# Retention rows turned in 32x32 blocks by VectorE during attention, in place of TensorE transposes in the output projection

## The reference

```python
ret = head_norm(ret).reshape(b, l, RET_HEADS * RET_DV) * jax.nn.silu(rg)
fox = forgetting_attention(heads(fq, FOX_HEADS), heads(fk, FOX_HEADS), heads(fv, FOX_HEADS), pad(logf))[:, PAD:]
mixed = jnp.concatenate([ret, fox], axis=-1).astype(h.dtype)      # 512 + 512 wide
return jnp.einsum('blc,cd->bld', mixed, w_out)
# then: h = layer_norm(ALPHA * h + that); router, shared expert, routed experts (top 6 of 64), layer norm
```

## Time and profile before

| | |
|---|---|
| median of 3 runs | 2919.52 us |
| the profiled execution | 2925.15 us |
| its span, first to last instruction | 2923.2 us |
| mean granted TensorE clock | 0.994 of full |
| TensorE busy | 2845.5 us, 97% |
| VectorE busy | 1679.1 us, 57% |
| ScalarE busy | 626.5 us, 21% |
| GpSimd busy | 1348.8 us, 46% |
| moved by DMA | 462.10 MB, mean 158 GB/s |

### The profile page before, as it was taken

The page is one execution under the profiler, slowest core; times in us unless marked ns, Lnnn a source line. Parts: engine busy times, 40 slices in busy tenths (PEclk is TensorE's granted clock), DMA queues, the critical chain, the costliest instruction groups (busy, mean ns, idle before and its releaser), DMA issues.

```text
span 2923.2 us, 40626 instructions
## 1 busy us (share of the span) xinstructions
PE 2845.5 (97%) x14506; PEld 2078.4 (71%) x14506; DVE 1679.1 (57%) x4553; ACT 626.5 (21%) x1285; POOL 1348.8 (46%) x1140
## 2 busy tenths in 40 slices
PE   8999999999999999998999999999999999999997
PEld 4478888888875555554555767778877777777775
DVE  6665556654246666664577644677677773332326
ACT  2221122120015455543111100111111111111114
POOL 3433534447740110101245435677667766555645
PEclk9999999999999999999999999999999999999999
DMA  6500110101020103003543466899899989999986
GB/s 221 183 6 1 31 45 1 30 15 44 15 88 7 54 8 117 13 7 125 187 152 119 154 225 204 268 280 276 270 279 284 292 277 307 301 306 305 315 256 254
DMA packets 181019, 462.10 MB, mean 158 GB/s; under 512 B 26072, under 2 KB 98600, under 8 KB 155080
## 3 DMA queue, kind: packets, MB, share of 16 engines
q1 hardware_dynamic: 133872, 339.23, 32.3%
q0 software_dynamic: 44640, 111.84, 16.6%
q10 hardware_dynamic: 2304, 8.39, 0.7%
HBM read 345.44 MB, written 113.92 MB: 157 GB/s over the span
## 4 chain that ended last, share of the span: by engine, by line
PE 39%; DMA 7%; DVE 3%; POOL 2%; issue 1%; ACT 0%; SPq 0%; DVEq 0%; POOLq 0%; ACTq 0%
PE ps L3005 17%; PE ps L2775 8%; DMA moe_xg<-t_rows,index 6%; PE ps L2948 4%; PE ps L2919 3%; PE ps L2831 2%; DVE moe_xT L2060 2%; PE ps L2916 2%; POOL moe_xg L2484 1%; DMA base_rows<-moe_yo,index 1%; PE ps L2841 1%; PE ps L2794 1%; POOL moe_fin L2566 1%; PE ps L2785 0%; DVE moe_yo L2115 0%
## 5 line engine op out<-in xcount | busy, mean ns | idle before, releaser
L2484 POOL DMA_INDIRECT moe_xg<-t_rows,index x433 | 422.7, 976 | 166.9 <-issue 119.8
L3005 PEld LDWEIGHTS ps<-moe_xT,moe_wg 128*128 128x128 f32 x2048 | 352.4, 196 | 49.4 <-issue 28.4
L3005 PE MATMUL ps<-moe_xT,moe_wg 128*128 128x192 f32 (+22 forms) x2048 | 378.7, 338 | 4.7 <-DVE moe_hh L1960 4.7
L3005 PE MATMUL ps<-moe_xT,moe_wu 128*128 128x192 f32 (+22 forms) x2048 | 375.3, 336 | 0.0
L2505 POOL DMA_INDIRECT base_rows<-moe_yo,index x100 | 235.9, 2359 | 266.5 <-DVE moe_yo L2074 124.1
L3005 PEld LDWEIGHTS ps<-moe_xT,moe_wu 128*128 128x128 f32 x2048 | 353.3, 196 | 4.3
L2060 DVE STREAM_TRANSPOSE moe_xT<-moe_xg 128x256 f32<-128x256 f32 x433 | 235.1, 609 | 189.2 <-DMA moe_xg<-t_rows,index 159.3
L1274 POOL TENSOR_TENSOR fox_diag<-fox_c,fox_causal 128x128 f32<-128x128 f32 x128 | 55.8, 458 | 449.7 <-DVE fox_mx L1303 444.9
L2625 ACT ACTIVATE moe_sl<-ps 128x256 f32<-128x256 f32 (+19 forms) x144 | 49.8, 346 | 917.3 <-PE ps L3005 827.7
L1297 DVE CUSTOM_DVE_ANT_0 hT<-ps,fox_c 128x512 f32<-128x512 f32 (+7 forms) x320 | 166.4, 560 | 67.1 <-PE ps L1543 66.8
L2115 DVE SCALAR_TENSOR_TENSOR moe_yo<-ps,weight,moe_yo 128x512 f32<-128x512 f32 (+14 forms) x280 | 187.5, 742 | 28.3 <-ACT moe_yo L2648 28.3
(11 more groups left out here) (371 smaller groups left out, 5035.8 us busy)
## 6 DMA issues: line engine op xcount, KB each, us to landing
moe_wg<-in_we_gate SPq DMA_DIRECT2D x64, 1024.0 KB
moe_wu<-in_we_up SPq DMA_DIRECT2D x64, 1024.0 KB
moe_wd<-in_we_down SPq DMA_DIRECT2D x64, 1024.0 KB, 8.9
fox_c<-ck SPq DMA_DIRECT2D x8, 1032.0 KB, 8.9
emb_xin<-in_x SPq DMA_DIRECT2D x16, 512.0 KB, 3.9
h_rows<-emb_hr SPq DMA_DIRECT2D x16, 512.0 KB, 2.8
ret_w<-in_w_in SPq DMA_DIRECT2D x16, 512.0 KB, 6.6
moe_yt<-h_rows SPq DMA_DIRECT2D x16, 512.0 KB, 4.8
```

What stands on the lines that cost most here:

```text
L2484: pool.indirect_dma_start(out=xg[g % NXG][:, :], out_offset=None, in_=quarters, in_offset=bass.IndirectOffsetOnAxis(ap=route.index4[:, AT4 ...
L3005: ins = pe.matmul(out, w[:, c, f:FF:FC], xT[u][:, c, 0:n], start=(c == 0), stop=(c == DC - 1))
```

## The change

The transposes of the retention rows leave TensorE and the output projection. During attention, in the first four tiles of each pair (`TURN_AT`), the 16 blocks are turned one by one: SP loads the rows of a block in four pieces, one for each head, onto four bands of 32 partitions (`rows_to_turn`); VectorE turns them in blocks of 32x32 with one instruction (`turn_rows`); SP stores the result in a new DRAM array `mT_rows`. Turning by bands of 32 leaves features 4p to 4p + 3 on partition p, not p, p + 128, ...; the first half of `w_out` is loaded in that order (`quartered`). The projection then loads `mT` straight from `mT_rows`. `turn_mix` and `mT_copy` are gone, and `mixes(i + 3)` stands right behind `feathers(i + 3)`.

```diff
             def projection_weights():
-                natural = w_out.rearrange("(c p) n -> p c n", p=P)
+                quartered = w_out[0:RH * RD, :].rearrange("(p c) n -> p c n", c=RH)
+                natural = w_out[RH * RD:MIX, :].rearrange("(c p) n -> p c n", p=P)
...
+                sp.wait_ge(rows_out, 16 * 2)
                 for b in range(2):
-                    sp.dma_start(ahead.mix[b][:, :], mixed[P * b:P * (b + 1), :]).then_inc(ahead.mix_in[b], 16)
+                    sp.dma_start(ahead.mT[b][:, :, :], mT_rows[b].rearrange("p (c t) -> p c t", c=RH)).then_inc(ahead.mix_in[b], 16)
+
+            def rows_to_turn(m):
+                for h in range(RH):
+                    sp.dma_start(ahead.turn_in[QP * h:QP * (h + 1), :, :],
+                                 mixed[P * m:P * (m + 1), RD * h:RD * (h + 1)].rearrange("(g t) d -> t g d", t=QP)
+                                 ).then_inc(rows_in, 16)
...
+            sp.wait_ge(added, PRODUCTS * len(FUNITS))
+            rows_to_turn(0)
             pair_gates(1)
             for n, (p, t) in enumerate(order):
+                if n in TURN_AT:
+                    m = TURN_AT[n]
+                    sp.wait_ge(rows_turned, m + 1)
+                    sp.dma_start(mT_rows[m], flat(ahead.turn_out[:, :, :])).then_inc(rows_out, 16)
+                    if m + 1 < NX:
+                        rows_to_turn(m + 1)
                 if n == 2 * TILES + 1:
                     projection_weights()
...
+            def turn_rows(m):
+                dve.wait_ge(rows_in, 16 * RH * (m + 1))
+                if m >= 1:
+                    dve.wait_ge(rows_out, 16 * m)
+                dve.transpose(ahead.turn_out[:, :, :].rearrange("p c (g t) -> p g c t", t=QP),
+                              ahead.turn_in[:, :, :].rearrange("p g (t c) -> p g c t", c=RH)).then_inc(rows_turned, 1)
...
                     if i == 1 and n >= 1:
                         finish(n - 1)
+                    if i == 2 and n in TURN_AT:
+                        turn_rows(TURN_AT[n])
...
             def mixes(i):
-                if i >= 2:
-                    sp.wait_ge(mturned, i - 1)
-                sp.dma_start(mix[i % 2][:, :], rows(mixed, i)).then_inc(mix_in[i % 2], 16)
+                sp.wait_ge(projected, 2 * (i - 2) + 2)
+                sp.dma_start(mT[i % 2][:, :, :], mT_rows[i].rearrange("p (c t) -> p c t", c=RH)).then_inc(mix_in[i % 2], 16)
...
-            mixes(2)
             sp.dma_start(sgu[:, :, 0:FF], natural(ws_gate)).then_inc(sw_s, 16)
...
                     feathers(i + 3)
+                    mixes(i + 3)
                     hidden(i + 3)
-                if i + 4 < NX:
-                    mixes(i + 4)
...
             def project(i, a):
                 if a == 0:
-                    pe.wait_ge(mT_a, i + 1)
+                    pe.wait_ge(mix_in[i % 2], 16 * (i // 2 + 1))
...
             def rank(i):
                 pe.wait_ge(chain, chosen_at[i])
-                pe.wait_ge(mT_a, min(i + 5, NX))
...
                     pe.wait_ge(counted_in, i)
+                    pe.wait_ge(slotted, i)
...
-            turn_mix(0)
             for i in range(-2, NX - 2):
                 project(i + 2, 0)
                 if i >= 0:
                     turn_t(i)
-                if i < 0:
-                    turn_mix(i + 3)
                 project(i + 2, 1)
-                if 0 <= i < NX - 3:
-                    turn_mix(i + 3)
```

More of the change, by code:

```diff
@@ L222, in __init__ @@
         sb = Area(nc, "moe", (self.rows, self.small))
-        self.mix = [sb(f"mix{b}", [P, RH * RD]) for b in range(2)]
+        self.mT = [sb(f"mT{b}", [P, RH, P]) for b in range(2)]
+        self.turn_in, self.turn_out = sb("turn_in", [P, NQ, P]), sb("turn_out", [P, RH, P])
         self.base, self.wo_at = self.rows, self.low
@@ L1099, in retention_phase, with fox_phase @@
         yield
-def fox_phase(nc, ps, ident, hT, square, w_in, w_out, v_rows, ck, mixed, foxT, ahead):
+def fox_phase(nc, ps, ident, hT, square, w_in, w_out, v_rows, ck, mixed, mT_rows, foxT, ahead):
     with Phase(nc, "fox") as ph:
@@ L1193, in fox_phase @@
         ahead.fox_proj, ahead.q_scaled, ahead.fox_wsum, ahead.fox_tsum = proj, zero("q_scaled"), zero("wsum"), zero("tsum")
+        rows_in, rows_turned, rows_out = zero("rows_in"), zero("rows_turned"), zero("rows_out")
+        TURN_AT = {TILES * p + x: TILES // 2 * p + x for p in range(PAIRS) for x in range(TILES // 2)}
         scored, biased, bounded, exped, diag_set = (zero(n) for n in ("scored", "biased", "bounded", "exped", "diag_set"))
@@ L1223, in projection_weights @@
             def projection_weights():
[L1224 removed]
+                quartered = w_out[0:RH * RD, :].rearrange("(p c) n -> p c n", c=RH)
+                natural = w_out[RH * RD:MIX, :].rearrange("(c p) n -> p c n", p=P)
                 sp.wait_ge(scored, unit0[2 * TILES])
                 for a in range(2):
[L1227 to L1228 removed]
+                    half = slice(a * BANK, (a + 1) * BANK)
+                    sp.dma_start(ahead.wo[:, 0:RH, half], quartered[:, :, half]).then_inc(ahead.wo_s[a], 16)
+                    sp.dma_start(ahead.wo[:, RH:MIX // P, half], natural[:, :, half]).then_inc(ahead.wo_s[a], 16)
+                sp.wait_ge(rows_out, 16 * 2)
                 for b in range(2):
[L1230 removed]
+                    sp.dma_start(ahead.mT[b][:, :, :], mT_rows[b].rearrange("p (c t) -> p c t", c=RH)).then_inc(ahead.mix_in[b], 16)
[4 more added lines that the diff above has]
+                                 ).then_inc(rows_in, 16)
             sp.wait_ge(proj, pair_done(0))
@@ L1685, in __init__, with moe_phase @@
         self.ones_set = ctx.enter_context(nc.semaphore("ones_set"))
-def moe_phase(nc, ps, mixed, foxT, h_rows, w_out, ln_g, ln_b, w_router, router_bias, ws_gate, ws_up, ws_down,
+def moe_phase(nc, ps, mT_rows, foxT, h_rows, w_out, ln_g, ln_b, w_router, router_bias, ws_gate, ws_up, ws_down,
               we_gate, we_up, we_down, t_rows, tT_rows, base_rows, table, route, ln2_g, ln2_b, out, square, ahead):
@@ L1769, in moe_phase @@
         zrow = sb("zrow", [P, D])
-        mix = ahead.mix
+        mT = ahead.mT
         fT = [sb(f"fT{b}", [P, PAIRS, P]) for b in range(2)]
         rows0 = spans[-2] - 4 * PAIRS * P
-        mT = [sb(f"mT{b}", [P, RH, P]) for b in range(2)]
         tT = [sb(f"tT{b}", [P, DC, P]) for b in range(2)]
@@ L1820, in moe_phase @@
         t_out, tT_out, scat = ph.zero_sems("t_out", NYT), ph.zero_sems("tT_out", 2), ph.zero_sems("scat", 2)
-        mturned, mT_a, projected, summed, stats, aggr, centred, epsd, rstds, t_ready = (
-            zero(n) for n in ("mturned", "mT_a", "projected", "summed", "stats", "aggr", "centred", "epsd", "rstds", "t_ready"))
+        projected, summed, stats, aggr, centred, epsd, rstds, t_ready = (
+            zero(n) for n in ("projected", "summed", "stats", "aggr", "centred", "epsd", "rstds", "t_ready"))
         halved, halved_c, fold_set = (zero(n) for n in ("halved", "halved_c", "fold_set"))
@@ L3059, in build @@
     mixed, foxT = dram("mixed", (SEQ, RH * RD)), dram("foxT", (FH * FD, SEQ))
+    mT_rows = dram("mT_rows", (NX, P, RH * P))
     t_rows, base_rows = dram("t_rows", (SEQ + SPARE, D)), dram("base_rows", (SEQ + SPARE, D))
@@ L3069, in build @@
                   retention_phase(nc, ps, ident, hT, a["square"], a["w_in"], a["retc"], v_rows, ck, mixed, ahead),
-                  fox_phase(nc, ps, ident, hT, a["square"], a["w_in"], a["w_out"], v_rows, ck, mixed, foxT, ahead)]
+                  fox_phase(nc, ps, ident, hT, a["square"], a["w_in"], a["w_out"], v_rows, ck, mixed, mT_rows, foxT, ahead)]
         for stage in stages:
@@ L3077, in build @@
         route = Route(nc, ctx, ident)
-        moe_phase(nc, ps, mixed, foxT, h_rows, a["w_out"], a["ln1_g"], a["ln1_b"], a["w_router"], a["router_bias"],
+        moe_phase(nc, ps, mT_rows, foxT, h_rows, a["w_out"], a["ln1_g"], a["ln1_b"], a["w_router"], a["router_bias"],
                   a["ws_gate"], a["ws_up"], a["ws_down"], a["we_gate"], a["we_up"], a["we_down"], t_rows, tT_rows,
```

9 lines of the change are left out of this document (1 added, 8 removed).

## The result

| | before | after |
|---|---|---|
| median of 22 runs each, taken in turn | 2924.85 us | 2931.48 us |
| lowest and highest | 2917.69 to 2937.86 | 2924.46 to 2943.59 |
| the profiled execution | 2925.15 us | 2931.47 us |
| its span | 2923.2 us | 2929.6 us |
| mean granted clock | 0.994 | 0.992 |

After over before is 1.0021 (95% interval 1.0011 to 1.0031): 6.6 us slower by the medians, by the interval 3 to 9. The forecast was +5.4 us, and 2924.9 as the time.

What follows compares the result with a forecast made beforehand. TensorE was taken to bound both the attention tiles and the output projection. Attention +7.1, third block +2.0 by landing and +2.0 by the clock, thirteen groups -5.7 give +5.4 us on 2919.52: 2924.9 us, range 2914.5 to 2930.

Steps and rivals of the forecast that it cites:

- The level: Whole run: the summed change of +5.4 us was put on a median of 2919.52 us, giving 2924.9.
- Attention: Sixteen VectorE transposes in the four largest tiles of each head pair delay TensorE 1.8 us a pair, 7.1 us in all.
- Tile 0 and 3: First and fourth attention tile of a pair: the later VectorE copy costs TensorE nothing.
- tile 1: Second attention tile of a pair: the copy moves 1.1 us later and TensorE stands for 0.7 us.
- tile 2: Third attention tile of a pair: TensorE already waits for this copy, so the whole 1.1 us is felt.
- These rivals: Attention transposes: at the copy's rate, 2922 us, chance 0.09; or strided reads twice as slow, 2935 us, chance 0.09.
- Third block: Output projection: `mT` lands behind 3 MB, TensorE waits 3.8 us, and the product starts 2.0 us later than before.
- The lag of 0.3 us: Third block's load in the projection: a consumer starts some 0.3 us after the landing.
- the head of the stage: Start of the output projection: removing the first group and its copy, 1.8 us at the lower clock, counted as 0.9.
- The clock in that wait: TensorE idle before the third block loses its clock: 2.0 us, ends 0 and 3.1; no loss had chance 0.14.
- Thirteen groups: Projection from the third block on: removed groups of TensorE transposes save 13 x 0.44 = 5.7 us.
- Nothing for `rank`, the row loads and `w_out`: The wait that `rank` gets, the turns' row loads and the split `w_out` load are hidden and cost nothing.

Runs made afterwards that it cites:

- after again: A second profiled execution of the unaltered changed kernel: attention 514.44 us, projection 388.96, experts 1092.70, tail 79.86.
- e1: Changed kernel with each VectorE turn moved from behind the bias of group 2 to ahead of the bias of group 0: 2923.02 us, ratio to before 0.9990.
- e5: Changed kernel with eight unused TensorE product instructions put ahead of the third block's products, to fill the wait for `mT`: 2931.39 us in one run.
- e6: Changed kernel with every block turned twice on VectorE, the second time over the first: attention 541.10 us, 26.7 more than after.
- e2: Changed kernel with the three loads of the shared expert's weights (3 MB) sent behind block 2's loads: 2923.57 us, ratio to before 0.9989.
- e3: Changed kernel with both the turns ahead of the bias of group 0 and the shared weights behind block 2's loads: 2919.45 us, ratio to before 0.9975.
- before again: A second profiled execution of the unaltered kernel before: 2941.23 us, 14.9 of the 16 us more lying in the experts.

## Why the prediction was near in the change and wrong in the time

- **The level, the step that failed.** "On the median the sum gives 2924.9" put +5.4 on the median of three runs, 2919.52. Twenty-two runs of the same kernel have their median 5.3 us higher, at 2924.85, and spread over 20 us, not "some 5". The forecast change on the right level would have been 2930.2, against 2931.48. The profile shown already stood 5.6 above that median; the text noted it and went by the three. The range was made of the bounds of the terms and of the rivals, with nothing for the level. The repeated executions put most of the spread in the routed experts: 1089.9 and 1104.8 us for one kernel.
- **Attention, +7.1 expected, +6.6 measured.** Right place by place. Tile 0 and 3 nothing; tile 1 0.7 expected, 0.60 later in the trace; tile 2 1.1 expected, 1.0 more wait (1.16 less 0.15). The duration, scaled from the transposes half as large, was 1.06; it is 1.12 to 1.22 with its end, and pushes the copy by 1.07. By an estimate from the rule of the Trainium skill (Vector Engine (DVE) Microarchitecture Reference, section 3.8: one element per cycle and lane) and from the rate of the copy, it would have been about 0.6 us. The runs disagree with it by a factor of nearly two: all 16 of 128x512 have a median of 1136 ns. The strided read costs nothing that can be seen, since twice the elements of the earlier trace rows take about twice the 0.53 us. These rivals fall.
- **Third block, +2.0 by landing expected, +0.45 measured.** This term was mis-sized. The wait was forecast at 3.8 and is 3.70, but by two errors that cancel: counted from the stage's start, the load was forecast to land at 34.2 us and lands at 32.9, and TensorE was forecast to come at 30.8 and comes at 29.3. The lag of 0.3 us from landing to consumer was misread, too: TensorE was busy with other products until 1389.03 and did not wait for that landing, and in after the lag is 0.1. The product comes 32.95 us behind the stage's start, where before it came 32.50. The other four executions with this order (after again, e1, e5, e6) have 34.20, 33.20, 33.56 and 33.16, so +0.45 to +1.7, against +2.0. On the other side the head of the stage came 2.5 us shorter, not 0.9 (to the first `fT` products 5.05 us, 7.59 before), and that rests on luck with the low clock: the first run of eight is 5.16 to 6.70 us long over six executions that are alike up to there, and 5.99 in before. Where TensorE waits for the load anyway, what is gained at the head goes into that wait. This is why e1, e2 and e3 are read from the head's end on.
- **The clock in that wait, 2.0 expected, 1.8 measured**, and 2.6 in after again. e5 shows that it goes with the idle time. It was not certain: e1 waited 3.13 us and lost nothing.
- **Thirteen groups, -5.7.** Right: a pass is 16.50 us, and from the third block to the experts 348.78 us where before took 354.44, 5.66 less.
- **Nothing for `rank`, the row loads and `w_out`.** Right: e1 has them all, and its attention is 0.15 us longer than before.

With the measured terms: 6.6 + 0.45 + 1.8 - 5.7 = +3.2, and the two stages differ by 6.63 - 3.42 = +3.2 us in the profiles, 2.2 less than the +5.4 forecast for them. The medians say +6.6 with an interval from 3 to 9. That +5.4 stands near this is in part luck: it owes as much to the 3.5 us that after's profile has more in the experts, for which the forecast had nothing. There one kernel alone differs by 15, and 1.4 of the 3.5 are busy time, with a stretch at a granted clock of 0.50 from 1933 us on, which before lacks and before again has at 1929; whether the change adds anything there is open. e3 speaks against much of it: it has the same `mT_rows` and the same turns, its two stages are 7.4 us shorter than before's, and the timed difference is 7.3.

## What to carry to other kernels

Work that is moved to an engine with slack is paid where it stands in that engine's list. Put it where the engine waits for the engine that sets the time (here ahead of the next tile's scores), not between a result and its consumer: the same 16 instructions cost 6.6 us at one place and 0.15 at the other. When a compute step is replaced by a load, the load's place in the queue is part of the change: with 3 MB in front of it that nobody needed yet, the run lost 5.6 us, against 7.5 that were to be won. And a forecast of a few us on a time of 3 ms must carry the spread of the level, which three runs don't show.

## What the runs showed of the hardware that I had not expected

- How long TensorE may idle before the clock falls isn't a matter of the one wait. In the projection, behind dense products, waits of 3.70, 3.79 and 3.99 us were followed by the granted clock 0.50 (the lower level, 1.2 GHz), one of 3.13 and one of 2.70 by 1.00; in the attention, where TensorE has other gaps, waits of 1.57 and 2.29 us (e6) were followed by 0.50, and those of 0.45 and 1.16 (after) by 1.00. The wait of 2.70 us for `moe_yo` had 1.00 around it in before and after, and 0.50 in e5. In after again the clock fell within the wait (0.51 from 1399.5 to 1401.0, the wait ends at 1401.38), in after only behind it.
- Behind nearly equal waits in the projection the low clock cost 1.8 us (after), 1.8 (e6) and 2.6 (after again).
- A VectorE transpose of 128x512 in 32x32 blocks, reading 16 bytes apart, takes 1.09 to 1.22 us, and the same instruction is some 0.04 us shorter at the place of e1.
- A load of 256 KB issued behind 3 MB landed 9.5 us after its issue, with the DMA engines at a share of 1.00 (after). Two of the three issues of these 3 MB held the queue's list for 7.46 and 3.63 us, where most take 0.4 to 0.7.
